# Queries and keys with the tokens as stationary side, and nine narrow fillers ahead of the experts

## The reference

```
def diff_attention(h, w_in, q_gain, k_gain, lam_params, subln_w, w_out, rel_bias, lambda_init):
    q, k, v = jnp.split(h @ w_in, 3, axis=-1)
    q = rms_norm(q.reshape(b, s, ATTN_HEADS, 2, d), q_gain).transpose(3, 0, 2, 1, 4)
    k = rms_norm(k.reshape(b, s, ATTN_HEADS, 2, d), k_gain).transpose(3, 0, 2, 1, 4)
    ...
    logits = einsum('bhqd,bhkd->bhqk', q, k) * d ** -0.5 + bias      # d = 64
    attn = softmax(logits of q1, k1) - lam * softmax(logits of q2, k2)
    o = rms_norm(attn @ v, subln_w) * (1 - lambda_init)
    return o @ w_out
...
logits = t @ router                       # t: the 256 normed tokens
top_logits, top_idx = lax.top_k(logits, 2)
out = sum over 8 experts of combine[:, e] * ((silu(t @ w_gate[e]) * (t @ w_up[e])) @ w_down[e])
```

## Time and profile before

| | |
|---|---|
| median of 3 runs | 1549.72 us (1549.19 to 1550.11) |
| the profiled execution, its own time | 1549.13 us |
| its span | 1547.3 us |
| PE busy | 1522.6 us, 98% of the span |
| DVE busy | 1314.8 us, 85% |
| ACT busy | 1108.8 us, 72% |
| chain that ended last | 57% PE's issue, 33% PE; DVE 4%, ACT 3% |
| mean granted clock of PE | 0.997 |

### The profile page before, as it was taken

One profiled execution on the slowest core, in us unless ns is written; L12 is line 12 of the kernel. 1 busy time (PEld: TensorE's weight loads), 2 busy tenths in 40 slices (PEclk: granted clock), 3 DMA queues, 4 the chain that ended last, 5 costly groups with the idle time before them and its releaser, 6 DMA issues.

```text
span 1547.3 us, 23711 instructions
## 1 busy us (share of the span) xinstructions
PE 1522.6 (98%) x8561; PEld 1313.5 (85%) x8561; DVE 1314.8 (85%) x1555; ACT 1108.8 (72%) x1331; POOL 68.9 (4%) x66
## 2 busy tenths in 40 slices
PE   9999999999999999999999999999999999999997
PEld 7879899999999997888888888888888888888885
DVE  6766777777798769999999999999999999999995
ACT  6776444445678757888788788788788788888884
POOL 2001100010010000000000000000000000000000
PEclk9999999999999999999999999999999999999998
DMA  9335445455343379999999999999999999999980
GB/s 349 115 135 197 164 167 209 169 202 176 114 165 133 138 296 394 377 387 379 386 391 360 386 392 352 388 393 353 393 388 351 394 388 351 393 388 351 394 309 12
DMA packets 189043, 455.70 MB, mean 295 GB/s; under 512 B 4321, under 2 KB 5573, under 8 KB 188976
## 3 DMA queue, kind: packets, MB, share of 16 engines
q1 hardware_dynamic: 185472, 444.29, 77.6%
q0 software_dynamic: 3360, 10.44, 2.6%
q10 hardware_dynamic: 144, 0.07, 0.0%
HBM read 449.52 MB, written 5.26 MB: 294 GB/s over the span
## 4 chain that ended last, share of the span: by engine, by line
issue 57%; PE 33%; DVE 4%; ACT 3%; POOL 2%; DMA 1%; SPq 0%; POOLq 0%; DVEq 0%; ACTq 0%
PE bank L702 32%; ACT split_mem L1219 1%; POOL mem L676 1%; DVE split_mem L1682 1%; POOL out L668 1%; DMA h_rows<-mem 1%; ACT mem L1342 0%; DVE mem L1893 0%; ACT L1178 0%; DVE mem L1868 0%; DVE split_mem L2256 0%; DMA mem<-x 0%; ACT mem L1343 0%; ACT mem L1355 0%; DVE mem L1710 0%
## 5 line engine op out<-in xcount | busy, mean ns | idle before, releaser
L702 PE MATMUL bank<-split_mem 128*128 128x512 f32 (+1 forms) x7680 | 1440.7, 348 | 4.9 <-ACT mem L1343 1.4
L702 PEld LDWEIGHTS bank<-split_mem 128*128 128x128 f32 x7680 | 1223.8, 189 | 188.0 <-issue 6.3
L2256 DVE TENSOR_TENSOR split_mem<-mem,split_mem 128x1024 fp32r<-128x1024 f32 x668 | 806.0, 1222 | 66.0 <-ACT split_mem L1565 24.7
L1565 ACT CAST split_mem<-mem 128x1024 fp32r<-128x1024 f32 x672 | 705.2, 1051 | 189.8 <-PE bank L702 188.2
L1682 DVE TENSOR_TENSOR split_mem<-mem,split_mem 128x1024 fp32r<-128x1024 f32 x172 | 214.6, 1255 | 88.9 <-ACT split_mem L1219 88.5
L1219 ACT CAST split_mem<-mem 128x1024 fp32r<-128x1024 f32 x172 | 177.9, 1044 | 140.5 <-PE bank L702 138.8
L702 PE MATMUL bank<-mem 128*64 128x256 f32 (+7 forms) x306 | 38.0, 328 | 2.8 <-DVE mem L1614 1.5
L1572 ACT ACTIVATE mem<-bank,small 96x512 f32<-96x512 f32 x56 | 38.4, 685 | 2.1 <-DVE small L2201 2.1
L2263 DVE TENSOR_TENSOR mem<-mem,bank 96x512 f32<-96x512 f32 x56 | 37.9, 676 | 0.0
L702 PEld LDWEIGHTS bank<-mem 128*64 128x64 f32 (+2 forms) x306 | 29.4, 168 | 8.4 <-issue 4.0
L1868 DVE SCALAR_TENSOR_TENSOR mem<-mem,colA 128x253 f32<-128x253 f32 (+2 forms) x72 | 31.9, 484 | 3.8 <-ACT mem L1308 2.3
(11 more groups left out here) (215 smaller groups left out, 490.8 us busy)
## 6 DMA issues: line engine op xcount, KB each, us to landing
mem<-moe_w_gate SPq DMA_DIRECT2D x56, 2048.0 KB, 9.4
mem<-moe_w_up SPq DMA_DIRECT2D x56, 2048.0 KB, 9.6
mem<-moe_w_down SPq DMA_DIRECT2D x56, 2048.0 KB, 9.8
mem<-ssd_w_in SPq DMA_DIRECT2D x10, 2048.0 KB, 7.9
mem<-ffn_w_gate SPq DMA_DIRECT2D x7, 2048.0 KB, 8.5
mem<-ffn_w_up SPq DMA_DIRECT2D x7, 2048.0 KB, 8.1
mem<-ffn_w_down SPq DMA_DIRECT2D x7, 2048.0 KB, 8.1
mem<-attn_w_in SPq DMA_DIRECT2D x4, 2048.0 KB, 13.7
```

The lines of the kernel that those rows point to most:

```text
L702: return nc.tensor.matmul(o, lhsT, rhs, start=start, stop=stop, skip_group_check=shared)
L1565: nc.scalar.copy(wsplit[:, EXPERT_BUFFER[n % SPLITS], 0, :].rearrange("p (k n) -> p k n", n=w.shape[2]), quarter(w, q)).then_inc(w_hi, 1)
L2256: tt_(lo, quarter(w, q), hi.bitcast(F32), ALU.subtract).then_inc(w_lo, 1)
```

## The change

Queries and keys are projected like the values (`project_tokens`): the tokens are the stationary side and 512 weight columns move, 12 products for a quarter. The result has tokens on the partitions, so a group of 64 lies along the free axis. ACT squares straight from the bank with the token's rate as scale (step 4t+4), DVE sums groups of 64 with two reductions (step 4t+5), ACT makes Ln and Exp of 128x16 numbers (step 4t+5), DVE multiplies the banks by the 16 rates of each token (step 4t+6), PE turns the result with transposes of 128x128 (steps 7, 11, 15, 16, 19; in two banks' worth for a tile), and ACT brings each bank to its place with the gain (same steps). The constant `mean_hd` goes. Ahead of the experts nine products of 192 and 96 columns of the fast type stand in place of three float32 ones of 256.

```diff
-RAW_SCALE_AT = {4 * t + 4: t for t in range(4)}
-SQUARES_AT = {4 * t + 5: t for t in range(4)}
-QK_MEAN_AT = {4 * t + 6: t for t in range(4)}
-QK_SCALE_AT = {7: 0, 11: 1, 16: 2, 19: 3}
-QK_MEAN_BANK = [6, 6, 0, 2]
+SQUARES_AT = {4 * t + 4: t for t in range(4)}
+QK_MEAN_AT = {4 * t + 5: t for t in range(4)}
+QK_SCALE_AT = {4 * t + 6: t for t in range(4)}
+QK_TURN_AT = {7: (0, 1), 11: (2, 3), 15: (4,), 16: (5,), 19: (6, 7)}
+QK_TURN_BANK = [6, 7, 6, 7, 7, 7, 7, 6]
...
 # PE
+            def project_tokens(tile, banks, q, fresh=None):
+                inputs(banks, q, fresh)
+                for j in range(2):
+                    w = parts(tile, q, j)
+                    k = 2 * q + j
+                    for tt in range(TT):
+                        a_h, a_l = (h2[:, part, k, tt * P:(tt + 1) * P] for part in range(2))
+                        o = bank[banks[tt]][:, :]
+                        mm(o, a_h, w[0], k == 0, False)
+                        mm(o, a_l, w[0], False, False)
+                        last = mm(o, a_h, w[1], False, k == KD - 1)
+                last.then_inc(w_used, 1)
...
-                if at in QK_MEAN_AT:
-                    for hf in range(2):
-                        i = 2 * QK_MEAN_AT[at] + hf
-                        B.claim(pe, ("qk_ms", i))
-                        pe.wait_ge(qk_sq, i + 1)
-                        B.finish(mm(bank[B.at["qk_ms", i][0]][:, :], C("mean_hd"), sqb[:, hf, :], True, True), ("qk_ms", i))
+                for i in QK_TURN_AT.get(at, ()):
+                    t, hf = i // 2, i % 2
+                    B.claim(pe, ("qk_turned", i))
+                    for tt in range(TT):
+                        B.released(pe, ("qk", 2 * t + tt))
+                    for h in (2 * hf, 2 * hf + 1):
+                        for tt in range(TT):
+                            at_ = (h % 2) * T + tt * P
+                            last = nc.tensor.transpose(bank[QK_TURN_BANK[i]][:, at_:at_ + P],
+                                                       qn[:, t % 2, tt, h * P:(h + 1) * P], C("ident" if t % 2 else "anti"))
+                    B.finish(last, ("qk_turned", i))
...
-                    pe.wait_ge(qk_done, 4 if h < 4 else 8)
+                    for i in ((0, 1, 2, 3) if h < 4 else (4, 5, 6, 7)):
+                        B.released(pe, ("qk_turned", i))
...
-            keep_busy(3, 3, T)
+            narrow = in2[1][:, 0, 0, :]
+            for width in (192, 192, 192, 192, 96, 96, 96, 96, 96):
+                mm(bank[3][:, 0:width], narrow[:, 0:P], narrow[:, 0:width], True, True)
...
 # ACT
                 if at in SQUARES_AT:
+                    t = SQUARES_AT[at]
+                    act.wait_ge(rstd_ready, 1)
+                    if t:
+                        act.wait_ge(qk_sum, t)
+                    for tt in range(TT):
+                        B.ready(act, ("qk", 2 * t + tt))
+                        fn(sqb[:, tt, :], bank[2 * (t % 2) + tt][:, :], ACT.Square, scale=rstd[:, T + tt:T + tt + 1])\
+                            .then_inc(qk_sq, 1)
...
                 if at in QK_MEAN_AT:
+                    t = QK_MEAN_AT[at]
+                    act.wait_ge(qk_sum, t + 1)
+                    s = qst[:, t % 2, :, :]
+                    chain.link(fn(s, s, ACT.Ln, bias=C("eps"), scale=1.0 / HD))
+                    fn(s, s, ACT.Exp, scale=-0.5).then_inc(qk_rstd, 1)
+                for i in QK_TURN_AT.get(at, ()):
...
+                    B.ready(act, ("qk_turned", i))
+                    gain = colB[:, K_GAIN:K_GAIN + 1] if t % 2 else small[:, 25:26]
+                    B.release(fn((kT if t % 2 else qT)[:, h:h + 2, :],
+                                 bank[QK_TURN_BANK[i]][:, :].rearrange("p (a t) -> p a t", a=2), ACT.Identity, scale=gain),
+                              ("qk_turned", i))
...
 # DVE
+                if at in QK_MEAN_AT:
+                    t = QK_MEAN_AT[at]
+                    for tt in range(TT):
+                        dve.wait_ge(qk_sq, 2 * t + tt + 1)
+                        last = V_.tensor_reduce(qst[:, t % 2, tt, :], sqb[:, tt, :].rearrange("p (g d) -> p g d", d=HD),
+                                                AX_X, ALU.add)
+                    last.then_inc(qk_sum, 1)
                 if at in QK_SCALE_AT:
                     t = QK_SCALE_AT[at]
+                    dve.wait_ge(qk_rstd, t + 1)
...
+                    link(tt_(qst[:, t % 2, :, :], qst[:, t % 2, :, :], rstd[:, T:T + TT].unsqueeze(2).broadcast_to([P, TT, 8]),
+                             ALU.mult))
+                    for tt in range(TT):
+                        B.ready(dve, ("qk", 2 * t + tt))
+                        B.release(tt_(qn[:, t % 2, tt, :].rearrange("p (g d) -> p g d", d=HD),
+                                      bank[2 * (t % 2) + tt][:, :].rearrange("p (g d) -> p g d", d=HD),
+                                      qst[:, t % 2, tt, :].unsqueeze(2).broadcast_to([P, 8, HD]), ALU.mult), ("qk", 2 * t + tt))
```

More of the change, by code:

```diff
@@ L79, in constants @@
     put("mean_d", 1.0 / D)
-    put("mean_hd", (i[:, None] // HD == i[None, :] // HD) / HD)
     put("mean_v", 1.0 / P)
@@ L751, in keep_busy, with inputs @@
                     mm(bank[b][:, 0:width], C("ident"), moving[:, 0:width], True, True)
-            def project(tile, banks, q, fresh=None):
+            def inputs(banks, q, fresh):
                 if fresh == 0 and q == 0:
@@ L765, in project @@
                     pe.wait_ge(h_lo, 4 * fresh + q + 1)
+            def project_tokens(tile, banks, q, fresh=None):
[10 more added lines that the diff above has]
+                last.then_inc(w_used, 1)
+            def project(tile, banks, q, fresh=None):
+                inputs(banks, q, fresh)
                 for j in range(2):
@@ L874, in _ @@
                             B.claim(pe, ("qk", i) if t < 4 else ("v", i - 8))
[L875 to L887, removed]
+                    project_tokens(tile, (2 * (t % 2), 2 * (t % 2) + 1), q, 0 if t == 0 else None)
             for t in range(2):
@@ L1235, in attention @@
                 if at in SQUARES_AT:
[L1236 to L1240, removed]
-                        fn(sqb[:, hf, :].rearrange("p (a t) -> p a t", a=2), qk_at(i), ACT.Square).then_inc(qk_sq, 1)
+                    t = SQUARES_AT[at]
[6 more added lines that the diff above has]
+                            .then_inc(qk_sq, 1)
                 if at in V_AT:
@@ L1244, in attention @@
                 if at in QK_MEAN_AT:
[L1245 to L1252 removed]
+                    t = QK_MEAN_AT[at]
[3 more added lines that the diff above has]
+                    fn(s, s, ACT.Exp, scale=-0.5).then_inc(qk_rstd, 1)
+                for i in QK_TURN_AT.get(at, ()):
+                    t, h = i // 2, 4 * (i // 4) + 2 * (i % 2)
+                    if i == 0:
+                        act.wait_ge(lam_ready, 1)
+                        B.released(act, "rowsB")
+                    B.ready(act, ("qk_turned", i))
[3 more added lines that the diff above has]
+                              ("qk_turned", i))
                 if at in TURN_AT:
@@ L1747, in attention @@
                     last.then_inc(attn_ready, 1)
-                if at in RAW_SCALE_AT:
-                    t = RAW_SCALE_AT[at]
-                    dve.wait_ge(rstd_ready, 1)
-                    for hf in range(2):
-                        i, h = 2 * t + hf, 4 * (t // 2) + 2 * hf
-                        B.ready(dve, ("qk", i))
-                        out = kT[:, h:h + 2, :] if t % 2 else turned(qT[:, h:h + 2, :])
-                        src = two(bank[2 * (t % 2) + hf][:, :])
-                        rate = rstd[:, 0:T].unsqueeze(1).broadcast_to([P, 2, T])
-                        if t % 2 == 0:
-                            src, rate = (v.rearrange("p a (b t) -> p a b t", b=TT) for v in (src, rate))
-                        B.release(tt_(out, src, rate, ALU.mult), ("qk", i))
+                if at in QK_MEAN_AT:
[5 more added lines that the diff above has]
+                    last.then_inc(qk_sum, 1)
@@ L1760, in attention @@
                 if at in QK_SCALE_AT:
                     t = QK_SCALE_AT[at]
-                    dest, gain = (kT, colB[:, K_GAIN:K_GAIN + 1]) if t % 2 else (qT, small[:, 25:26])
-                    for hf in range(2):
-                        i, h = 2 * t + hf, 4 * (t // 2) + 2 * hf
-                        dve.wait_ge(qk_rstd, i + 1)
-                        stt(out=dest[:, h:h + 2, :], in0=dest[:, h:h + 2, :], scalar=gain, in1=two(rq[:, hf, :]),
-                            op0=ALU.mult, op1=ALU.mult).then_inc(qk_done, 1)
+                    dve.wait_ge(qk_rstd, t + 1)
```

28 lines of the change are left out of this document (8 added, 20 removed).

## The result

| | before | changed |
|---|---|---|
| median of 7 runs each | 1549.27 us (1547.55 to 1550.11) | 1554.72 us (1552.41 to 1556.02) |
| ratio | | 1.0033, interval 1.0024 to 1.0042 |
| profiled execution, its span | 1549.13 us, 1547.3 us | 1554.87 us, 1553.0 us |
| mean granted clock of PE | 0.997 | 0.996 |
| PE busy | 1522.6 us | 1521.4 us |

The changed kernel is slower by 0.33%, 5.45 us. The forecast was 1551.1 us (+1.4 against before); the median lies 0.2 us above the range's upper end of 1554.5, where the case "the clock falls twice" (1554.3) stood. "Within 0.2%" was given 0.66, "slower" 0.24.

A forecast was written before the change was run, and what follows sets the result against it. PE, busy for 98% of the span, was taken as the bound. Its work of -5.6 us plus waits of 2.8, 0.9, 3.5 and -0.1 made +1.5 (+1.4 unrounded): median 1551.1 us, range 1548.5 to 1554.5.

The forecast's parts named there:

- the clock falls twice: PE's clock drops behind the gaps of steps 7 and 15, giving 1554.3 us; half of the clock rival's 0.24.
- Within 0.2%: Whole kernel: median between 1546.6 and 1552.8 us, not distinguishable from no change; chance 0.66.
- slower: Whole kernel: median above 1552.8 us, through clock falls, a longer chain or a late gather; chance 0.24.
- The waits: PE idle ahead of the turning at steps 7, 11 and 15, for 2.8, 0.9 and 3.5 us.
- The walk: Instruction-by-instruction timing through the queues of PE, ACT and DVE up to step 20; difference trusted to about 1 us.
- both rivals about the chain's length: Reductions of 0.84 us make waits longer (1552.9 us, chance 0.08), or of 0.42 us shorter (1549.5 us, 0.10).
- PE's own work: Attention stage: products -0.3 and -1.9, means -6.9, turning +3.5, together -5.6 us.
- Tile 0: Two quarters of the first tile become shorter through the new form of products: -0.3 us.
- Forecast as walked, clock kept: Whole kernel: the walked waits come and PE's clock stays up, median 1551.1 us; chance 0.48.
- The clock: Rival: PE's clock falls in the gaps of steps 7 and 15, 1.6 us each; chance 0.24.
- Fillers: Ahead of the experts' gather: the narrow products end before it may start, 0 us; 0.65 us kept for the range.
- No new wait: Rival: DVE and ACT finish before PE at steps 7, 11 and 15, giving 1544.1 us; chance 0.10.

The follow-up runs named there:

- Experiment 5: Changed kernel with DVE's sums and rates queued ahead of a head's weights within a step; 1551.01 us, ratio 1.0012 to the kernel before.
- experiment 1: Changed kernel with the three float32 fillers of before in place of the nine narrow ones; 1554.00 us, ratio 1.0024 to the kernel before.
- experiment 0: Changed kernel run again without edit, as reference on another chip; 1554.46 us, ratio 1.0030 to the kernel before.
- experiment 4: Changed kernel with the first tile's turning at step 8 in place of 7; 1551.90 us, ratio 1.0016 to the kernel before.
- 3: Changed kernel with unread float32 products ahead of the turning, two at step 7 and three at step 15; 1552.20 us, ratio 1.0015 to the kernel before.
- 9: Changed kernel with three unread float32 products ahead of the turning of step 15 alone; 1551.83 us, ratio 1.0017 to the kernel before.
- 6: Changed kernel with first turning at step 8, DVE's sums and rates ahead of weights, and the old fillers; 1547.83 us, ratio 0.9992 to the kernel before.
- 8: Changed kernel with first turning at step 8 and DVE's sums and rates ahead of weights, narrow fillers kept; 1548.46 us, ratio 0.9994 to the kernel before.
- 10: The kernel of 6 run once more, on the same chip as 8; 1548.10 us, ratio 0.9992 to the kernel before.
- Experiment 7: Changed kernel with PE turning the constant identity without waiting for DVE; routing changes, so only the stage to step 20 is readable; 3448.86 us, ratio 2.23.
- experiment 2: Kernel before with only the nine narrow fillers added in place of its own; 1550.69 us, ratio 1.0007 to the kernel before.

## Why the prediction was right and wrong

**The waits: right.** The walk gave 2.8, 0.9 and 3.5 us; PE's brackets show 2.71, 1.02 and 3.13, and in terms of loads, which is what the time pays, 3.06, 1.37 and 3.48, together 7.9 for 7.2. PE's brackets are 0.3 us below the walk in sum; the loads show about 0.35 us more than the brackets at each of the three places, 1.05 in all, where a stream of 512-column products is cut. The walk had no term for that. The waits are ended by what the walk named. The groups of instructions by shape:

```profile
L1778 DVE TENSOR_TENSOR mem<-bank,mem 128x512 f32<-128x512 f32 x8 | 5.2, 686 | 0.1
L1765 DVE TENSOR_REDUCE mem<-mem 128x8 f32<-128x512 f32 x8 | 5.1, 679 | 0.0
L1249 ACT ACTIVATE mem<-bank,rstd 128x512 f32<-128x512 f32 x8 | 5.1, 684 | 2.7 <-PE bank L699 2.7
...
L1257 ACT ACTIVATE mem<-mem,cst 128x16 f32<-128x16 f32 x4 | 1.2, 308 | 9.5 <-DVE mem L1765 9.5
L1258 ACT ACTIVATE mem<-mem 128x16 f32<-128x16 f32 x4 | 0.9, 217 | 0.1
```

The reduction, which no row of before showed, takes 0.68 us, as taken; so both rivals about the chain's length fall. The order at step 15 can be read off DVE and ACT:

```profile
61.39 1.27 DVE L1765 TENSOR_REDUCE mem<-mem 128x8 f32<-128x512 f32 x2
...
66.14 0.75 DVE L1757 SCALAR_TENSOR_TENSOR mem<-mem 128x128 f32<-128x128 f32 x2
66.81 0.17 DVE L1774 TENSOR_TENSOR mem<-mem,rstd 128x16 f32<-128x16 f32 x1
67.01 1.29 DVE L1778 TENSOR_TENSOR mem<-bank,mem 128x512 f32<-128x512 f32 x2
```

```profile
62.70 0.31 ACT L1257 ACTIVATE mem<-mem,cst 128x16 f32<-128x16 f32 x1 [3.78 <-DVE mem L1765]
63.04 0.22 ACT L1258 ACTIVATE mem<-mem 128x16 f32<-128x16 f32 x1
63.16 0.39 ACT L1280 ACTIVATE mem<-mem 128x128 f32<-128x128 f32 x1
```

ACT stands 3.78 us before its Ln with head 1's exponentials queued behind it; DVE's weights of head 1 need these, and the rates stand behind the weights. Experiment 5 takes that link out, and the wait goes.

**PE's own work: right.** Loads of a quarter are 0.225 us apart for 0.227; a turning of eight takes 0.82 us from its start to the next product's, four tiles 3.3 for 3.5; the means are gone. The stage without a fall is 2.2 us longer, for 1.7 walked (the 1.4 without tile 0's -0.3) and the 0.7 of waits above the walk.

**Tile 0: wrong, 0.8 us.** Forecast -0.3, measured +0.5. Its first quarter took 3.93 us (9.20 to 13.13) for 3.34. PE was slow at the start as in the earlier trace rows: products of 512 columns took 628 ns up to the one that starts at 11.1 us, and 389 or a little more from 11.8 on, while before the pace had doubled by 9.9. The walk had them at the full pace. The products of that line around and behind the change of pace (durations min/median/max in ns, first and last start):

```profile
L699 PE MATMUL bank<-split_mem x8: 389/390/628, 11.1 to 12.9; 128*128 128x512 f32 x8
```

The start itself moves by more than that between executions (the mean of the first norm begins at 24.28 to 26.44 us in the profiles of the experiments with the same tile 0), so one pair of profiles says little of it.

**The clock: the step that failed.** "Forecast as walked, clock kept: 0.48", against 0.24 for a fall. The price of a fall, 1.6 us, was right for the two falls of the changed kernel (1.56 at step 15, 1.63 in the gather); those of experiment 1 cost 2.8 and 2.6, so it isn't a fixed price. The longest gap, named first, was the place of the first fall. What failed is the argument against it: "both have dense work before and behind, the 2.9 us had none behind". Dense work behind doesn't save the clock. In all four profiles with the gap of 3.1 us at step 15 (the changed kernel, 0, 1, 4) it fell, in three of them when the dense work had begun again 0.7 to 1.1 us before. Where the gap is filled (3, 9) or short (5, 6, 8, 10) it did not. Experiment 9 shows it as a cause: same delay, no stillness, no fall in the profile, and 2 to 2.5 us less by the ratios, though their intervals overlap. The mean granted clock of all executions says the same, profiled or not: of the 40 with the 3.1 us gap (changed, 0, 1, 4) none reaches 0.998, of the 66 with it filled or short (3, 9, 5, 6, 8, 10) 51 do. The gap of 2.7 us at step 7 was followed by a fall in one of the five profiles that have it unfilled (1; not the changed kernel, 0, 5, 9).

The Trainium skill, page "TensorE: Matmul & The Clock Gate", section "HAM oscillation — how this bites in real kernels", says that idle gaps between bursts of matmuls bring the clock down; these traces agree for step 15. With its Part 4, "PE-mode transpose" (transposes don't count as activity in the same way), I had worked out two falls, at steps 7 and 15, and 1554.3 us. The time came out near that, but by falls at step 15 and in the gather, so the agreement is luck: at step 7, where that reading wanted one, four of five profiles have none. No run here separates transposes from the other work.

**The second fall: its place was not foreseen.** It was in the gather in two of the four profiles with a fall at step 15 (three of the four have narrow fillers, and both are among these), and in none of the others. Experiment 7, which has a fall too (at step 16) and the narrow fillers, has none in the gather. Two explanations stay open: that the narrow fillers, which end 0.28 us ahead of the gather and don't fill the time as the old ones did, make it possible there, or that it has to do with the fall 515 us before. The first has for it that all falls in the gather stand behind narrow fillers; so has the mean clock of 0.996 in four of experiment 2's eleven executions, for one of 33 of the kernel before. Against it, 8 and 2 show no cost beyond their intervals, and their profiles no fall. Neither was shown.

**Fillers: right as far as can be told.** Nine in 1.19 us, 0.13 each or less; the gather starts no later; at most 0.0007 in any pair. Whether they make a fall in the gather more frequent is the open question above.

**"No new wait": not to be had with the queues in this order.** It stood at 0.10 with 1544.1 us. Experiment 7 shows why it didn't come: with the waits taken out, DVE's weights become the bound at steps 15 to 17. The case's condition named three places; a fourth limit stood behind them. Whether another order of DVE's queue would remove that limit too was not tried. In 6 the 1.2 us that are won come from putting the waits where less is lost by them.

The sum as it should have stood: 1549.13 + 2.2 (stage) + 0.5 (start) + 1.6 (step 15) = 1553.4 with one fall, and with 1.75 from the gather on 1555.2 with two, for 1552.92 and 1554.87 measured (the first is the profile of experiment 0, from another set of runs). The 0.3 left in the second is in the rest of the kernel.

## What to carry to other kernels

When a change takes 5 us from an engine that is always busy and puts a round trip through two others in front of it, walk the round trip through their queues; the gain went into 7.9 us of waits at three places here. Then ask of every wait near 3 us what the clock does behind it: a gap of 3.1 us cost its own length and another 1.6, once 2.6, though dense work followed. The remedies were cheap and measured: queue the late result's producer ahead of work that isn't due (2.8 us), move the consumer one step back (2.2 us), or, where neither can be had, let the engine do work that nobody reads in the gap (2.0 to 2.3 us). Each figure is a difference of two ratios to experiment 0 and uncertain by some 2 us; the two first together, 5.9 us below experiment 0, are clear of that.

## What the runs showed of the hardware

- The clock fell up to 1.1 us after PE had started again (69.6 against 68.45), so a fall is to be looked for behind a gap, not only in it. In experiment 1 both falls came in the gap, 2.0 us after PE's last product. A stretch at 1.2 GHz lasted 3.4 us in the changed kernel and 6.8 in experiment 1, where it cost 2.6 to 2.8 us for 1.6.
- A gap of 1.94 us was also followed by one (experiment 7), and one of 2.7 us was followed by one in one profile of five: length alone doesn't decide.
- The executions of the changed kernel (experiment 0) fall into groups about 2 us apart, near the 1.6 us of one fall of the clock. For changes of a few us a fall is as large as the effect, and the mean granted clock of an execution is a hint whether to look for one: 0.997 or 0.998 in profiles without a fall ahead of PE's last product, 0.997 with one of 3.4 us, 0.996 with two, 0.993 with two of 6.8 us.
- The granted clock reads 1.00 at the start, where products of 512 columns take 628 ns for 389 behind; the moment at which the pace doubles varies: from its start to the next instruction, tile 0's first quarter took 3.26 us in experiments 6 and 10 and 4.44 in experiment 4, with the same work.
- DVE's sum over groups of 64 in 128x512 numbers takes 0.68 us, the same as a multiplication of that shape; a transpose of 128x128 float32 costs PE 0.10 us.
